# Differential attention on one core: the scores of a half in two matmuls on stacked operands instead of three, with k projected ahead of q

## What is computed

```python
qkv = jnp.einsum('bld,de->ble', h, w_in)
q, k, v = jnp.split(qkv, 3, axis=-1)
q = q.reshape(bsz, L, N_HEADS, 2, HEAD_DIM)      # 8 heads, 2 halves, 64
k = k.reshape(bsz, L, N_HEADS, 2, HEAD_DIM)
...
for qs, qe in _query_blocks(L):                  # 16, then 4 x 128
    s = jnp.einsum('bqhcd,bkhcd->bhcqk', q[:, qs:qe], k[:, :qe]).astype(jnp.float32) * scale
    ...
    p = jax.nn.softmax(s, axis=-1)
    a = (p[:, :, 0] - lam * p[:, :, 1]).astype(v.dtype)
    outs.append(jnp.einsum('bhqk,bkhe->bqhe', a, v[:, :qe]))
```

## Time and profile before

| | |
|---|---|
| median of 3 runs | 2024.48 us (2023.16 to 2024.65) |
| the profiled execution | 2022.77 us, of which the span from first to last instruction is 2021.0 us |
| mean granted TensorE clock | 0.984 |
| PE busy | 1935.2 us, 96% |
| PEld busy | 1684.3 us, 83% |
| DVE busy | 1054.7 us, 52% |
| ACT busy | 680.2 us, 34% |
| attention stage | from about 755 to 1008 us of the span |

### The profile page before, as it was taken

The page is one execution under the profiler, slowest core; times in us unless marked ns, Lnnn a source line. Parts: engine busy times, 40 slices in busy tenths (PEclk is TensorE's granted clock), DMA queues, the critical chain, the costliest instruction groups (busy, mean ns, idle before and its releaser), DMA issues.

```text
span 2021.0 us, 27462 instructions
## 1 busy us (share of the span) xinstructions
PE 1935.2 (96%) x11390; PEld 1684.3 (83%) x11390; DVE 1054.7 (52%) x1481; ACT 680.2 (34%) x959; POOL 171.2 (8%) x129
## 2 busy tenths in 40 slices
PE   7999899999999999999989999999899989999996
PEld 5876777888888778989889999999899868888885
DVE  7676746434434776666656333434555464343343
ACT  4555433222213344443434232323322243223131
POOL 3000023000000220000022000001300130000002
PEclk9999999999999999999999999999899999999998
DMA  4120121222222121111121222222122212222221
GB/s 177 63 104 21 53 84 63 94 94 102 86 105 104 65 103 63 43 43 43 63 84 63 84 98 91 97 90 83 67 97 87 105 63 87 101 95 92 99 88 42
DMA packets 25906, 166.05 MB, mean 82 GB/s; under 512 B 3792, under 2 KB 4048, under 8 KB 6352
## 3 DMA queue, kind: packets, MB, share of 16 engines
q1 hardware_dynamic: 25808, 164.66, 22.8%
HBM read 162.55 MB, written 2.10 MB: 81 GB/s over the span
## 4 chain that ended last, share of the span: by engine, by line
PE 85%; DVE 10%; ACT 2%; issue 1%; DMA 0%; POOL 0%; SPq 0%; ACTq 0%; DVEq 0%; POOLq 0%
PE ps L314 23%; PE ps L315 23%; PE ps L316 23%; PE ps L1971 2%; DVE z_lo L422 2%; DVE ps L471 2%; PE ps L1972 2%; PE ps L1973 2%; DVE h L484 2%; PE ps L2025 1%; DVE w_lo L296 1%; PE ps L1686 1%; PE ps L2079 1%; PE ps L1688 1%; PE ps L1687 1%
## 5 line engine op out<-in xcount | busy, mean ns | idle before, releaser
L314 PE MATMUL ps<-z_hi,w_hi 128*128 128x256 f32 (+1 forms) x1632 | 567.2, 348 | 35.5 <-DVE z_lo L422 35.3
L315 PE MATMUL ps<-z_lo,w_hi 128*128 128x256 f32 (+1 forms) x1632 | 562.9, 345 | 0.0
L316 PE MATMUL ps<-z_hi,w_lo 128*128 128x256 f32 (+1 forms) x1632 | 561.8, 344 | 0.0
L296 DVE TENSOR_TENSOR w_lo<-w_raw,w_hi 128x2048 fp32r<-128x2048 f32 x152 | 348.3, 2291 | 161.5 <-ACT w_hi L285 161.4
L285 ACT ACTIVATE w_hi<-w_raw 128x2048 fp32r<-128x2048 f32 x152 | 289.8, 1906 | 402.5 <-PE ps L316 382.9
L314 PE MATMUL ps<-arena,w_hi 128*128 128x512 f32 (+1 forms) x1140 | 389.8, 342 | 3.5 <-issue 1.9
L315 PE MATMUL ps<-arena,w_hi 128*128 128x512 f32 (+1 forms) x1140 | 389.9, 342 | 0.0
L316 PE MATMUL ps<-arena,w_lo 128*128 128x512 f32 (+1 forms) x1140 | 389.3, 341 | 0.0
L314 PEld LDWEIGHTS ps<-z_hi,w_hi 128*128 128x128 f32 x1632 | 312.4, 191 | 82.6 <-issue 29.6
L316 PEld LDWEIGHTS ps<-z_hi,w_lo 128*128 128x128 f32 x1632 | 312.2, 191 | 39.0
L315 PEld LDWEIGHTS ps<-z_lo,w_hi 128*128 128x128 f32 x1632 | 312.8, 192 | 37.6 <-issue 0.7
(11 more groups left out here) (296 smaller groups left out, 2038.2 us busy)
## 6 DMA issues: line engine op xcount, KB each, us to landing
w_raw<-wstream SPq DMA_DIRECT2D x152, 1024.0 KB, 4.8
h<-xT SPq DMA_DIRECT2D x8, 256.0 KB, 7.3
out<-h SPq DMA_DIRECT2D x8, 256.0 KB, 2.0
rope_cs<-pT SPq DMA_DIRECT2D x1, 512.0 KB, 5.6
acc<-pos SPq DMA_DIRECT2D x1, 256.0 KB, 2.7
acc<-lam SPq DMA_DIRECT2D x1, 128.0 KB, 9.1
sm<-small SPq DMA_DIRECT2D x1, 86.0 KB, 2.5
h<-metaT SPq DMA_DIRECT2D x1, 64.0 KB, 9.4
```

The costliest lines, as they stand in the source:

```text
L296: dve.tensor_tensor(w_lo[:, slot, :], w_raw[:, slot, :], w_hi[:, slot, :].bitcast(f32), ALU.subtract).then_inc(wlo, 1)
L314: pe.matmul(dst, wh, zh, start=(k == 0), stop=False)
L315: pe.matmul(dst, wh, zl, start=False, stop=False)
L316: last = pe.matmul(dst, wl, zh, start=False, stop=(k == nk - 1))
```

## The change

q's and k's operands are laid out by half. For q, tile `a_stack(0, c)` holds the half's high part in the 64 partitions of half c and its low part in the other 64. For k, `a_stack(1, c)` holds the half's high part twice. One matmul over 128 partitions then gives high x high + low x high. A second one over 64 partitions adds q's high with k's low, which lies in `a_klo`, a part of the output tiles' place. k's high copy becomes four copies of 64x528, q's two, and each low part two operations of 64x528. k is projected ahead of q, so the first tile taken is k; the semaphore targets follow. The diff, cut where it repeats:

```diff
-        def a_qk(part, which, hh):
-            at = A_2 + ((part * 2 + which) * 2 + hh) * T
+        def a_stack(which, c, hh):
+            at = A_2 + ((which * 2 + c) * 2 + hh) * T
             return arena[:, at:at + T]
+        def a_klo(hh):
+            return a_out(hh, KD - 1)
+        def half(c):
+            return slice(64 * c, 64 * c + 64)
...
-            def qk_hi(m, kind):
-                act.wait_ge(ps_free, 2 * P_QKV + 3 * m + kind + 1)
-                act.activation(a_qk(0, kind, m % 2), qkv_tmp(m, kind), ACT.Copy).then_inc(s("dq_hi"), 1)
+            def k_hi(m):
+                act.wait_ge(ps_free, 2 * P_QKV + 3 * m + 1)
+                for home in range(2):
+                    for c in range(2):
+                        act.activation(a_stack(1, c, m % 2)[half(c if home == 0 else 1 - c)], qkv_tmp(m, 0)[half(c)],
+                                       ACT.Copy).then_inc(s("dq_hi"), 1)
+            def q_hi(m):
+                act.wait_ge(ps_free, 2 * P_QKV + 3 * m + 2)
+                for c in range(2):
+                    act.activation(a_stack(0, c, m % 2)[half(c)], qkv_tmp(m, 1)[half(c)], ACT.Copy).then_inc(s("dq_hi"), 1)
...
-                    qk_hi(m, 0)
+                    k_hi(m)
...
-                    qk_hi(m, 1)
+                    q_hi(m)
...
-            def qk_lo(m, kind):
-                dve.wait_ge(s("dq_hi"), 2 * m + kind + 1)
-                dve.tensor_tensor(a_qk(1, kind, m % 2), qkv_tmp(m, kind), a_qk(0, kind, m % 2).bitcast(f32), ALU.subtract).then_inc(s("dq_lo"), 1)
+            def k_lo(m):
+                for c in range(2):
+                    dve.wait_ge(s("dq_hi"), 6 * m + c + 1)
+                    dve.tensor_tensor(a_klo(m % 2)[half(c)], qkv_tmp(m, 0)[half(c)], a_stack(1, c, m % 2)[half(c)].bitcast(f32),
+                                      ALU.subtract).then_inc(s("dq_lo"), 1)
+            def q_lo(m):
+                for c in range(2):
+                    dve.wait_ge(s("dq_hi"), 6 * m + c + 5)
+                    dve.tensor_tensor(a_stack(0, c, m % 2)[half(1 - c)], qkv_tmp(m, 1)[half(c)], a_stack(0, c, m % 2)[half(c)].bitcast(f32),
+                                      ALU.subtract).then_inc(s("dq_lo"), 1)
...
-                    q_take(m)
+                    kv_take(m, 0)
...
-                    qk_lo(m, 0)
+                    k_lo(m)
...
-                    kv_take(m, 1)
+                    q_take(m)
...
-                    qk_lo(m, 1)
+                    q_lo(m)
...
+                q = a_stack(0, c, n % 2)[:, q0:q0 + P]
+                if low:
+                    return pe.matmul(dst, q[half(c)], a_klo(n % 2)[half(c), a:e], start=False, stop=True)
+                return pe.matmul(dst, q, a_stack(1, c, n % 2)[:, a:e], start=True, stop=False)
...
                 if b == 0:
-                    pe.wait_ge(s("dq_lo"), 2 * n + 2)
+                    pe.wait_ge(s("dq_lo"), 4 * n + 4)
...
                 for c in range(2):
-                    d_pass(u, c, 0, 0, 0, e, True, False)
+                    d_pass(u, c, False, 0, e)
                 for c in range(2):
-                    d_pass(u, c, 0, 1, 0, e, False, False)
-                for c in range(2):
-                    d_pass(u, c, 1, 0, 0, e, False, True).then_inc(s("d_s"), 1)
+                    d_pass(u, c, True, 0, e).then_inc(s("d_s"), 1)
...
                 for a, e in cuts_of(T):
-                    d_pass(u, c, 0, 0, a, e, True, False)
-                    d_pass(u, c, 0, 1, a, e, False, False)
-                    last = d_pass(u, c, 1, 0, a, e, False, True)
+                    d_pass(u, c, False, a, e)
+                    last = d_pass(u, c, True, a, e)
...
-    qkv = [col(w_in_2[0], kind * D + n * P) for n in range(DIFF_HEADS) for kind in range(3)]
+    qkv = [col(w_in_2[0], kind * D + n * P) for n in range(DIFF_HEADS) for kind in (1, 0, 2)]
```

More of the change, by code:

```diff
@@ L960, in _ @@
             act_load(act, ACT.Exp)
-            qk_hi(0, 0)
-            qk_hi(0, 1)
+            k_hi(0)
+            q_hi(0)
             d_exp(0, 0)
@@ L1465, in q_take @@
             def q_take(m):
-                dve.wait_ge(ps_full, 2 * P_QKV + 3 * m + 1)
-                dve.scalar_tensor_tensor(qkv_tmp(m, 0), q_tile(3 * m), -SC2, rr[:, 0, :], op0=ALU.mult, op1=ALU.mult).then_inc(ps_free, 1)
+                dve.wait_ge(ps_full, 2 * P_QKV + 3 * m + 2)
+                dve.scalar_tensor_tensor(qkv_tmp(m, 1), q_tile(3 * m + 1), -SC2, rr[:, 0, :], op0=ALU.mult, op1=ALU.mult).then_inc(ps_free, 1)
             def kv_take(m, kind):
@@ L1517, in _ @@
             d_bias(0)
+            kv_take(0, 0)
             q_take(0)
-            kv_take(0, 1)
-            qk_lo(0, 0)
-            qk_lo(0, 1)
+            k_lo(0)
+            q_lo(0)
             d_min(0, 0)
@@ L2017, in out2_end, with d_pass @@
                 project(pe, b % 2, (P_OUT2 + 6) % 2, 0, KD, late_part, NLATE, 2 * P_OUT2 + 10, by_tile=True)
-            def d_pass(u, c, x, y, a, e, start, stop):
+            def d_pass(u, c, low, a, e):
                 n, b = divmod(u, 5)
-                r = slice(64 * c, 64 * c + 64)
                 q0 = 0 if b == 0 else META + P * (b - 1)
                 dst = across(S_BANK, T)[:, a:e] if b == 4 else ps[:, S_BANK + c, a:e]
-                return pe.matmul(dst, a_qk(x, 0, n % 2)[r, q0:q0 + P], a_qk(y, 1, n % 2)[r, a:e], start=start, stop=stop)
+                q = a_stack(0, c, n % 2)[:, q0:q0 + P]
+                if low:
+                    return pe.matmul(dst, q[half(c)], a_klo(n % 2)[half(c), a:e], start=False, stop=True)
+                return pe.matmul(dst, q, a_stack(1, c, n % 2)[:, a:e], start=True, stop=False)
             def d_s(u):
```

## The result

| | before | after |
|---|---|---|
| median of 4 runs each | 2023.82 us | 2039.96 us (2038.77 to 2040.91) |
| the profiled execution, its span | 2022.77, 2021.0 us | 2040.91, 2039.1 us |

The ratio is 1.0081 (95%: 1.007 to 1.0093): slower, as forecast, but by 16.1 us where the working gave 8.2, and above the range. Both of its causes are in the trace. Each is larger than its term, and a third one had no term.

What follows compares the result with a forecast made beforehand. TensorE, busy 96% of the span, was taken to bound the kernel. Terms of 5.6 + 1.3 + 1.2 = +8.2 us, with the runs' median at 2024.5, gave 2032.7 us, 0.4% slower; range 2026.8 to 2037.

Steps and rivals of the forecast that it cites:

- the covered case: Rival: the added copies stay hidden and only block 4's +2.5 us is left, 2027.0 us; chance 0.14.
- 5.6 + 1.3 + 1.2 = 8.2: Added us: waits and block 4 in heads 2, 4, 6 (5.6); head 0 (1.3); block 4 in heads 1, 3, 5, 7 (1.2).
- the third rival: More waits than counted, from failed pairing or slower copies to other partitions: 2037 us or more; chance 0.10.
- slower copies: Copies to other partitions than their input's take longer, entering the odd heads' operand chain four times.
- failed pairing: Blocks 0 to 3: the two 64-row matmuls fail to run side by side after the full ones, +3.8 us.
- two switches before, the same after. Price 0: Score matmuls of blocks 0 to 3: three streams and two row-mode switches before and after, so no added time.
- 0.15 a half: Block 4: two steps fewer but four switches instead of two, at 0.20 us each, +0.155 us a half.
- 0.31: Block 4's added time in each head, in us; +2.5 us over eight heads.
- the rival of a free switch there: Steps between full and 64-row passes of one unit cost no switch: 13.4 us saved, 2017 us in all; chance 0.07.
- 4 x 0.53: ScalarE's added high copies: four back-to-back steps of 0.53 us, 2.1 us a head.
- 0.62: VectorE's step in us for each added low part, taken from back-to-back operations; 1.2 us a head.
- somewhat more: Bound on copy durations, above whole ones, where an output lies on other partitions than its input; no row showed it.

Runs made afterwards that it cites:

- e2: The kernel before with only the score matmuls in the new shapes (one over 128 rows, one over 64), its output not the right one: 2027.87 us, ratio 1.0021.
- e8: The kernel before with three needless 64x528 low parts on VectorE ahead of q's, for the odd heads' operands alone: 2035.9 us, ratio 1.007.
- e3: The changed kernel with 15 matmuls, their result overwritten, put in TensorE's wait before the first scores of heads 1, 3, 5 and 7: 2035.2 us, ratio 1.0059.
- e1: The kernel before with only the new copies and the old 64-row passes, k's second high copies going to an unread tile: 2032.51 us, ratio 1.0049.
- e4: The changed kernel with block 4's passes of a half in the order full, full, 64, 64: 2038.75 us, ratio 1.007.
- e7: The changed kernel with block 4 full passes first, k's second copies late, and half of q's low part on GpSimd except for the first head: 2032.01 us, ratio 1.0055.
- e10: The changed kernel itself, run once more: 2039.66 us, ratio 1.0086.
- e5: The changed kernel with k's two second-home high copies moved behind block 4's first exponential on ScalarE: 2031.21 us, ratio 1.0043.
- e6: The changed kernel with both k's second high copies late and block 4 in the order full, full, 64, 64: 2029.68 us, ratio 1.0035.
- e9: The changed kernel with block 4 full passes first, the weight block's high copy behind the third probability copy, k's second pair behind both exponentials: 2026.38 us, ratio 1.0014.

## Why the prediction was half right

**Direction, place and pattern held.** q's low part became what TensorE waits for in heads 0, 2, 4 and 6; the covered case (0.14) is out: the 64-partition copies cost whole durations. The forecast's sum was 5.6 + 1.3 + 1.2 = 8.2; the runs put some 12 us in its place and 4 to 6 on top. Three steps failed: two terms were too small, and the clock had none. The two alone would have given 2024.5 + 12.1 = 2036.6, within the range; the clock put the time above it. That the time lies where the third rival had it, at 2037 or more, is half luck: its slower copies are near to what was found, but its failed pairing isn't in the trace, where the two 64-row matmuls of a block still start together (at 927.15 and 911.75), and it had nothing of the clock.

**Blocks 0 to 3, "two switches before, the same after. Price 0": wrong.** The count was right, but not where the switches lay. TensorE's timeline around block 3 of head 4, before:

```profile
900.66 0.28 PE L1973 MATMUL ps<-z_hi,w_lo 128*128 128x264 f32 x1
900.98 0.82 PE L2025 MATMUL ps<-arena 64*128 64x400 f32 x6
901.73 0.39 PE L1971 MATMUL ps<-z_hi,w_hi 128*128 128x264 f32 x1
901.96 0.29 PE L1972 MATMUL ps<-z_lo,w_hi 128*128 128x264 f32 x1
```

and after:

```profile
910.87 0.29 PE L1997 MATMUL ps<-z_hi,w_lo 128*128 128x264 f32 x1
911.19 0.63 PE L2051 MATMUL ps<-arena 128*128 128x400 f32 x2
911.75 0.45 PE L2050 MATMUL ps<-arena 64*128 64x400 f32 x2
912.12 0.39 PE L1995 MATMUL ps<-z_hi,w_hi 128*128 128x264 f32 x1
912.35 0.28 PE L1996 MATMUL ps<-z_lo,w_hi 128*128 128x264 f32 x1
```

Both units are entered with a step of 0.32 us from the matmul before. Before, the change from 128 to 64 rows lay inside that step and cost nothing more; now the first pass is full, the change comes behind it, and the unit takes 1.48 us instead of 1.30. Block 2 had the same luck, entered from the transposes of 16 rows without a switch: from its first score to the next other matmul it takes 0.77 instead of 0.57 us. Block 0 costs 0.10 more in the odd heads and 0.10 less in the even ones, block 1 nothing. Block 4 was sized rightly (0.15 a half). These make 0.6 and 0.8 a head, of which a part lies in waits: e2 measured 0.60 and 0.42 instead of 0.31, some 4 in all instead of 2.5. The rule of the Trainium skill that the prediction cites (TensorEngine Tiling (Array Packing), Key Properties) held with its 0.20 us, and it held within a unit as well: the rival of a free switch there (0.07) is out.

**The steps between copies, "4 x 0.53" and "0.62": too small.** ScalarE's four copies start at 914.72, 915.37, 916.04 and 916.70, the weight block at 917.37: 0.65 to 0.67 a step, not 0.53. VectorE's two low parts start at 925.34 and 926.08, the next operation at 926.81: 0.73 each, not 0.62. An operation of 64 partitions is as long as one of 128, but where the start partition changes it isn't overlapped with its neighbour. So the probability copy comes 2.14 later (predicted 1.60), the long minimum 1.74 (1.26) and q's low part 2.58 (1.88), each from the start of k's copy; TensorE waits 1.98 more instead of 1.57, and in heads 2, 4 and 6 another 0.26 at the transposes of block 3. e8 shows which steps lose the overlap. The Trainium skill has a model of it in VectorE: DVE Perf Modes, section Two Vector instructions with no wait between them: an instruction is held until the earlier ones are through when an input or its output starts in another quadrant of 32 partitions than the last one read or written in that memory. All four steps of e8 agree with it (0.35 and 0.61 within the same start, 0.73 and 0.74 where it changes). ScalarE's steps, of which that section doesn't speak, show the same: 0.54 into k's first copy (from 914.18), 0.65 to 0.67 from there on. The prediction took the step from operations that all start at partition 0. It allowed "somewhat more" only where the output lies on other partitions than the input, and priced it in the bounds, not in the sum; the steps between copies that stay in their partitions (914.72 to 915.37) are as long.

What the two parts make together is seen in e3, where the clock is whole. From first scores to first scores, heads 2, 4 and 6 are 2.54, 2.59 and 2.72 us longer than before (1.88 was forecast), head 0 2.20 (1.3), heads 1, 3 and 5 0.54, 0.49 and 0.46 (0.31), and head 7 up to its last transposes 0.60: 12.1 in all, which is also what the medians of e3 give.

**The clock: no term.** The stretches at 1.2 GHz in heads 1, 3 and 7 cost 1.5, 3.0 and about 1.5 us (heads 1, 3 and 5 take 33.63, 35.14 and 32.14 us for the same work). e3 fills the waits and gets it back; e8 makes waits without the change and has one stretch behind a wait. In both traces of the changed kernel the stage is 18.1 and 18.0 us longer than before, 12.1 and 5.9 of clock; the medians say 16.1 and 16.5, by which the clock is nearer to 4. The two traces don't show where that difference arises. The prediction read 1.00 in the earlier trace rows and carried it over to a kernel with waits of 1.9 us in it.

**Open.** Why a wait of 1.9 us costs the clock in head 3 and not in heads 1 and 5, in both profiles, isn't settled. Ten stretches, in after, e1, e4, e7, e8 and e10, begin within 2 us behind the end of a wait with a pitch of 1.6 or more. The others do not: those of head 1 in after and e10 and those of e5, e6 and one of e2 begin 13.3 to 13.6 us behind a head's first scores, two of e4 15.0, and e2's second and e8's first elsewhere. e2 has two though it has no such wait; before, e3 and e9 have none in the stage. So that long waits cost clock is shown for the kernel as a whole by e3, and for the single stretch it is an argument. e2's share of them, some 0.8 us of the 4.8 in its median, is part of the cost of the form only if the form is their cause. No run separates this.

## What to carry to other kernels

Fewer matmuls aren't less time: count streams, and between them the changes of row mode; ask of each change whether it lay in a wait before. A copy split by partitions costs its whole duration twice, and the overlap besides wherever the start partition changes; if it stands in the queue ahead of what another engine waits for, the whole chain pays, and reordering that queue gave back most of it (e9). Where a change puts waits of about 2 us into a TensorE that had none, price the clock as well, by a row at the lower level: here it was a quarter to a third of the loss.

## What the runs showed of the hardware

- A change between 128-row and 64-row matmuls costs 0.20 us in each direction, also between two passes into the same bank; coming from 16-row transposes into 64-row passes there is none.
- The overlap of neighbouring operations, about 0.1 us on ScalarE and VectorE, is lost where the start partition changes between 0 and 64.
- A GpSimd subtraction of 64x528 took 2.27 us and stretched a like one on VectorE that started during it from 0.70 to 1.34, and in other heads a following one with a single SBUF input from 0.43 to 1.45; a copy from PSUM kept its 0.43.
- The clock fell to 1.2 GHz at the same three places in two executions of one kernel, for 3.4 or 6.8 us: 0.1 and 0.5 us behind the ends of two of its four waits of 1.7 to 1.9 us, and 13.5 us behind a third. With matmuls in the waits it didn't fall.
